# Two feed-forward down projections on one core: Strassen's seven half-block products in place of the plain product, with GpSimd adding the blocks

## What is computed

```python
def conv_ffn(h, w_up, conv_w, conv_b, w_down):
    S = h.shape[1]
    u = h @ w_up                                   # 1024 -> 2 * 2816
    up = jnp.pad(u, ((0, 0), (CONV_W - 1, 0), (0, 0)))
    u = conv_b + sum(conv_w[j] * up[:, j:j + S] for j in range(CONV_W))
    gate, val = jnp.split(u, 2, axis=-1)
    return (jax.nn.silu(gate) * val) @ w_down      # 2816 -> 1024

for layer in range(DEPTH):
    ...
    x = x + m
    x = x + conv_ffn(rms_norm(x, norm_ffn[layer]), f_w_up[layer], ...)
```

## Time and profile before

| | |
|---|---|
| median of 3 runs | 1197.97 us (1197.91 to 1198.34) |
| span of the profiled execution | 1195.8 us; the median of the runs is 2.2 us longer, which lies around the span |
| TensorE busy | 1189.6 us, 99% of the span |
| VectorE, ScalarE, GpSimd busy | 756.1, 561.5 and 202.0 us |
| granted TensorE clock | 1.00 throughout |
| HBM traffic | 96 GB/s over the span |

### The profile page before, as it was taken

How to read it: one execution, slowest core, us unless ns; L and a number is a source line. 1 busy time by engine, 2 the same in 40 slices (tenths; PEclk the granted TensorE clock), 3 DMA queues, 4 the chain that set the end, 5 groups by cost and what they waited for, 6 DMA issues and landing times.

```text
span 1195.8 us, 17325 instructions
## 1 busy us (share of the span) xinstructions
PE 1189.6 (99%) x6082; PEld 974.4 (81%) x6082; DVE 756.1 (63%) x1331; ACT 561.5 (47%) x936; POOL 202.0 (17%) x297
## 2 busy tenths in 40 slices
PE   9999999999999999999999999999999999999998
PEld 7768886778888888888888987988888888888887
DVE  6588967945766566563335998845766566563334
ACT  6554337845433333342225789945443333342321
POOL 0533546820000000000000467720000000000000
PEclk9999999999999999999999999999999999999999
DMA  7522231213332232213232210023332222213232
GB/s 270 185 89 90 71 107 53 73 53 106 110 127 79 105 105 73 102 54 105 90 103 93 88 37 2 2 71 106 107 122 87 105 105 70 105 53 106 88 105 105
DMA packets 26673, 110.84 MB, mean 93 GB/s; under 512 B 2896, under 2 KB 3280, under 8 KB 19456
## 3 DMA queue, kind: packets, MB, share of 16 engines
q1 hardware_dynamic: 26624, 110.21, 27.0%
HBM read 108.06 MB, written 6.33 MB: 96 GB/s over the span
## 4 chain that ended last, share of the span: by engine, by line
PE 97%; ACT 1%; DVE 1%; issue 0%; POOL 0%; DVEq 0%; ACTq 0%; POOLq 0%
PE ps L2164 29%; PE ps L2166 28%; PE ps L2165 28%; PE ps L1931 3%; PE ps L1915 3%; PE ps L1731 1%; PE ps L2130 1%; PE ps L1772 1%; PE ps L1802 1%; PE ps L1899 1%; ACT probs L837 1%; PE ps L1783 0%; PE ps L1739 0%; DVE probs L1308 0%; PE ps L1711 0%
## 5 line engine op out<-in xcount | busy, mean ns | idle before, releaser
L1188 DVE TENSOR_TENSOR w_lo<-raw,w_hi 128x1024 fp32r<-128x1024 f32 (+2 forms) x108 | 179.9, 1665 | 263.0 <-ACT w_hi L747 263.0
L747 ACT ACTIVATE w_hi<-raw 128x1024 fp32r<-128x1024 f32 (+2 forms) x118 | 170.9, 1448 | 222.1 <-PE ps L2166 221.8
L2164 PE MATMUL ps<-h_hi,w_hi 128*128 128x512 f32 x704 | 274.6, 390 | 0.0
L2166 PE MATMUL ps<-h_hi,w_lo 128*128 128x512 f32 x704 | 274.1, 389 | 0.0
L2165 PE MATMUL ps<-h_lo,w_hi 128*128 128x512 f32 x704 | 274.1, 389 | 0.0
L2164 PE MATMUL ps<-a_hi,w_hi 128*128 128x512 f32 x480 | 187.6, 391 | 0.0
L2166 PE MATMUL ps<-a_hi,w_lo 128*128 128x512 f32 x480 | 187.0, 390 | 0.0
L2165 PE MATMUL ps<-a_lo,w_hi 128*128 128x512 f32 x480 | 187.0, 390 | 0.0
L1011 ACT ACTIVATE cv<-u_in,vec 128x512 f32<-128x512 f32 x88 | 71.2, 816 | 182.7 <-DVE u_in L1501 180.6
L2164 PEld LDWEIGHTS ps<-h_hi,w_hi 128*128 128x128 f32 x704 | 132.2, 188 | 28.0 <-issue 0.7
L2165 PEld LDWEIGHTS ps<-h_lo,w_hi 128*128 128x128 f32 x704 | 132.2, 188 | 27.2
(11 more groups left out here) (234 smaller groups left out, 1618.6 us busy)
## 6 DMA issues: line engine op xcount, KB each, us to landing
raw<-in_f_up SPq DMA_DIRECT2D x44, 1024.0 KB, 4.8
raw<-in_f_w_down SPq DMA_DIRECT2D x44, 512.0 KB, 3.3
raw<-in_a_in_wide SPq DMA_DIRECT2D x12, 1024.0 KB, 4.9
bias_tiles<-bias_rows SPq DMA_DIRECT2D x1, 4096.0 KB, 20.3
raw<-in_a_w_out SPq DMA_DIRECT2D x8, 512.0 KB, 3.3
raw<-in_b_w_out SPq DMA_DIRECT2D x7, 512.0 KB, 3.3
xT<-in_xt SPq DMA_DIRECT2D x8, 256.0 KB, 7.0
raw<-in_a_in_wide SPq DMA_DIRECT2D x8, 256.0 KB, 7.1
```

What stands on the lines that cost most here:

```text
L747: sc.activation(w_hi[:, s, 0:n], raw[:, s, 0:n], ACT.Copy).then_inc(w_hi_done, 1)
L1188: dve.tensor_tensor(w_lo[:, s, 0:n], raw[:, s, 0:n], w_hi[:, s, 0:n].bitcast(F32), ALU.subtract)\
L2164: pe.matmul(dst, s_hi, m_hi, start=start, stop=False)
L2166: return pe.matmul(dst, s_lo, m_hi, start=False, stop=stop)
```

## The change

The down projection is computed as a product of 2 x 2 blocks by Strassen's scheme. For each pair of row tiles (even and odd, `G_PAIRS` = 11), the weight has four blocks of 128 rows by 512 output columns and the activation four blocks of 128 rows by 256 tokens. Seven products of sums and differences of blocks (`SEVEN`: column block of the weight, block of the activation, first PSUM bank) take the place of eight plain ones. Each has four matmul triples of 256 columns per pair and gathers in two PSUM banks over the 11 pairs. As seven need 14 banks, there are two phases: units 0 to 10 make M1, M3, M6 and M2, units 11 to 21 load the weights again and make M4, M5 and M7. The last two units run product by product. VectorE adds each finished product onto one or two quarters of the residual, M3 and M2 after ScalarE has copied them to `cv`.

GpSimd makes the sums of the weight blocks in place in the raw slots (three additions of 512 columns in the first phase, two in the second) and sums of the activation blocks (three of 256 per pair), VectorE the other activation sums (two of 256 per pair, in units listed in `SUMMED_IN`). A third raw slot, `raw2`, lies where `h_hi` and `h_lo` lie, so its first load waits until the up projection is done. The first stage of layer 1 takes its weights in eight pieces in a new order and waits for the banks by `g_out`. The semaphores of the feed-forward are shared between the layers.

```diff
+SEVEN = {"M1": (0, 0, 2), "M3": (1, 1, 0), "M6": (2, 3, 4), "M2": (3, 2, 6),
+         "M4": (2, 2, 2), "M5": (0, 1, 0), "M7": (1, 0, 4)}
+G_PAIRS = FT // 2
+G_UNITS = 2 * G_PAIRS
+G_PARTS = ((("M1", "M3"), ("M6", "M2")), (("M4",), ("M5", "M7")))
+SUMMED_IN = {**{i + 2: (i,) for i in range(G_PAIRS - 2)}, 4: (2, 9), 7: (5, 10)}
...
+            raw2 = sb("raw2", [P, SLOT], F32, scope)
...
-                with sp.Fori(0, FT // 2) as i:
-                    for s in range(2):
-                        load(U_DOWN[l] + 2 * i + s, down_v[l][2 * i + s], raw[:, s, 0:D], s)
+                for u in range(G_UNITS):
+                    r, k = u % 3, 2 * pair_of(u)
+                    if u == 2:
+                        sp.wait_ge(f_done, 2 * FT * l + 4 * UP_STEPS)
+                    else:
+                        sp.wait_ge(w_lo_done, U_DOWN[l] + u - (1 if u < 2 else 2))
...
+            def gate_sums(l, i):
...
+                pool.wait_ge(f_act, FT * l + 2 * i + 2)
+                pool.tensor_tensor(g_pair[i][:, 0:HS], even[:, 0:HS], odd[:, HS:S], ALU.add)
+                chain.then_wait(pool.tensor_tensor(g_pair[i][:, HS:S], even[:, HS:S], odd[:, HS:S], ALU.subtract))
+                pool.tensor_tensor(even[:, HS:S], even[:, 0:HS], even[:, HS:S], ALU.add).then_inc(g_pre, 1)
...
+            def weight_sums(l, u):
...
+                pool.wait_ge(g_raw[r], g_landed(l, u))
+                if first_of_two(u):
+                    chain.then_wait(pool.tensor_tensor(s0, s1, s3, ALU.add))
+                    chain.then_wait(pool.tensor_tensor(s3, s2, s3, ALU.add))
+                    pool.tensor_tensor(s2, s2, s1, ALU.subtract).then_inc(g_sum, 1)
+                else:
+                    chain.then_wait(pool.tensor_tensor(s0, s0, s1, ALU.add))
+                    pool.tensor_tensor(s1, s1, s2, ALU.subtract).then_inc(g_sum, 1)
...
+            def sums_of_layer(l):
+
+                for i in range(G_PAIRS - 1):
+                    gate_sums(l, i)
+                for u in range(4):
+                    weight_sums(l, u)
+                gate_sums(l, G_PAIRS - 1)
+                for u in range(4, G_UNITS):
+                    weight_sums(l, u)
...
+            def seven_hi(l, u, p):
...
+                sc.wait_ge(g_sum, G_UNITS * l + u + 1)
+                if u >= 2:
+                    last = 1 if u in (G_PAIRS, G_PAIRS + 1) else p
+                    sc.wait_ge(r_used[1], G_USED * l + 2 * (u - 2) + last + 1)
...
+            def seven_lo(l, u, p):
...
+                dve.tensor_tensor(w_lo[:, s, at], raws[u % 3][:, at], w_hi[:, s, at].bitcast(F32), ALU.subtract)\
+                    .then_inc(w_lo_done if p else g_lo_first, 1)
...
+                dve.tensor_tensor(g_lo[s][:, at], g_source(u, p), g_hi[s][:, at].bitcast(F32), ALU.subtract)\
+                    .then_inc(r_lo[1], 1)
...
+            def gate_differences(l, i):
...
+                chain.then_wait(dve.tensor_tensor(g_diff[:, (i + 8) % G_PAIRS], odd[:, 0:HS], even[:, 0:HS],
+                                                  ALU.subtract))
+                dve.tensor_tensor(odd[:, 0:HS], odd[:, 0:HS], odd[:, HS:S], ALU.add).then_inc(g_diffed, 1)
...
+            def onto(l, count, c, t, source, op):
+
+                x = x_quarter(c, t)
+                dve.wait_ge(g_out, 10 * l + count - 1)
+                dve.tensor_tensor(x, x, source, op).then_inc(g_out, 1)
...
                     elif last:
-                        lo(U_DOWN[l])
-                        act_lo(n, 0, 0)
-                        act_lo(n, 1, 1)
+                        seven_lo(l, 0, 0)
+                        seven_lo(l, 0, 1)
...
-            onto_residual(1, U_DOWN[0], FT)
+            seven_products(0)
...
+                for u in range(G_UNITS - 2):
+                    for p, names in enumerate(G_PARTS[0 if first_of_two(u) else 1]):
+                        wanted(u, p)
...
+                            for d in range(4):
+                                ins = one(name, u, d)
...
+                for name in ("M4", "M5", "M7"):
+                    for u in (G_UNITS - 2, G_UNITS - 1):
```

More of the change, by code:

```diff
@@ L545, in _ @@
             load_ffn(1)
-            for k in range(KD):
-                sp.wait_ge(x_new[4], k + 1)
+            for k in range(4, KD):
+                sp.wait_ge(x_new[4], k // 2 - 1)
                 sp.dma_start(out[:, k, :], xT[:, k, :]).then_inc(out_sem, 16)
-            sp.wait_ge(out_sem, 16 * KD)
+            sp.wait_ge(g_out, 20)
+            for k in range(4):
+                sp.dma_start(out[:, k, HS:S], xT[:, k, HS:S]).then_inc(out_sem, 16)
+            for k in range(4):
+                sp.wait_ge(x_new[4], 3 + k // 2)
+                sp.dma_start(out[:, k, 0:HS], xT[:, k, 0:HS]).then_inc(out_sem, 16)
+            sp.wait_ge(out_sem, 16 * 12)
         @block.gpsimd
@@ L977, in onto_residual @@
                     for b in range(2):
-                        hi(u0 + 2 * i + b + 2, (r_used[n], 2 * i + b + 1), D, b)
+                        hi(u0 + 2 * i + b + 2, (r_used[n], 2 * i + b + 1), D, b, n // 2)
                         act_hi(n, 2 * i + b + 2, b, False)
[L980 to L1000, removed]
@@ new lines, in onto_residual @@
+                half = unit_words(nxt) // 2
+                sc.wait_ge(w_raw[0], 8 * nxt - 16 - (NO_RAW if n else 0))
+                sc.activation(w_hi[:, 0, D:D + half], raw[:, 0, D:D + half], ACT.Copy).then_inc(w_hi_upper, 1)
+                order = ORDER[n_next]
+                for j, k in enumerate(order):
+                    features_hi(n_next, k, gain_at)
+                    if j >= 2:
+                        square_of(n_next, order[j - 2])
+                    if j == KD - 2:
+                        hi(nxt, (r_done[n], KD), half)
@@ L1476, in onto_residual @@
                     dve.tensor_tensor(xT[:, k, :], xT[:, k, :], ps[:, k, :], ALU.add).then_inc(x_new[n_next], 1)
[L1477 removed]
+                    if 0 < j < KD - 1:
                         prepare_lo(n_next, order[j - 1], gain_at)
[L1479 to L1487 removed]
+                lo(nxt, half)
@@ new lines, in into_second_layer @@
+            def into_second_layer():
+                gain_at = G_MIX + KD
+                down_piece_lo(0)
+                down_piece_lo(1)
+                m4_onto_upper(0)
+                onto(0, 8, 0, 0, bank_tiles("M4", 0, 4), ALU.add)
+                prepare_lo(2, 4, gain_at)
+                down_piece_lo(2)
+                dve.wait_ge(g_done, 4)
+                onto(0, 9, 0, 0, bank_tiles("M5", 0, 4), ALU.subtract)
+                onto(0, 10, 0, 1, bank_tiles("M5", 0, 4), ALU.add)
+                prepare_lo(2, 5, gain_at)
+                down_piece_lo(3)
+                prepare_lo(2, 6, gain_at)
+                prepare_lo(2, 7, gain_at)
+                dve.wait_ge(g_out, 10)
+                seven_last(0, 0, 2)
+                seven_last(0, 2, 4)
+                down_piece_lo(4)
+                prepare_lo(2, 0, gain_at)
+                down_piece_lo(5)
+                prepare_lo(2, 1, gain_at)
+                down_piece_lo(6)
+                prepare_lo(2, 2, gain_at)
+                down_piece_lo(7)
+                prepare_lo(2, 3, gain_at)
+                total_squares(2)
@@ L1490, in feed_forward, with into_output @@
+            def into_output():
+                m4_onto_upper(1)
+                onto(1, 8, 0, 0, bank_tiles("M4", 0, 4), ALU.add)
+                dve.wait_ge(g_done, 12)
+                onto(1, 9, 0, 0, bank_tiles("M5", 0, 4), ALU.subtract)
+                onto(1, 10, 0, 1, bank_tiles("M5", 0, 4), ALU.add)
+                seven_last(1, 0, 2)
+                seven_last(1, 2, 4)
             def feed_forward(l):
```

375 lines of the change are left out of this document (296 added, 79 removed).

## The result

The changed kernel takes 1262.14 us (median; 1260.22 to 1263.73) against 1197.97: the ratio is 1.0534, 95% interval 1.0519 to 1.0549. It is slower by 64 us; the forecast was 1245, slower by 47, with a range that reaches to 1275. Direction and place are right, the size is 17 us short.

A forecast was written before the change was run, and what follows sets the result against it. VectorE and GpSimd, excluding each other, bound the down stages: 17 + 63.9 + 56.5 + 4.3 = 141.7 us against 119.7; 2 x 22 + 2.5 = 46.5 on the median 1197.97 gives 1244.5, say 1245; range 1220 to 1275.

The forecast's parts named there:

- TensorE's part: Down projection, per layer: 924 matmuls of 256 columns at 0.12 us, 110.9 us, 8.8 less than before.
- No meeting: Rival, chance 0.10: VectorE's remainders slip into GpSimd's gaps, TensorE bounds the down stages, about 1185 us.
- A meeting: VectorE's two-SBUF-input operation against GpSimd's SBUF-reading one: costs the sum of both steps less 0.35, 1.02 us to VectorE.
- Step 1, the lead: Start of each down stage: VectorE turns to unit 2 about 17 us after the last up matmul.
- Step 2, units 2 to 10: First phase of each down stage: VectorE and GpSimd queues at 7.64 us a unit, 63.9 us after corrections.
- Step 3, units 11 to 21: Second phase of each down stage: 4.72 us a unit plus residual additions, less 3.4 for PSUM reads, 56.5 us.
- starved chain: Rival, chance 0.06: VectorE also waits for loads or ScalarE, one microsecond on each of 20 units, 1285 us.
- Clock: Forecast 1.00 in the down stages; rival, chance 0.03: pauses drop TensorE to 1.2 GHz, steps 0.24 us, about 1400 us.
- Step 4: End of each down stage: TensorE's 36 matmuls after the last remainder, 4.3 us.
- The ends: After the down stages: about 1.5 us of waiting into layer 1 and 1 us more at the output, 2.5 together.
- The gate sums: GpSimd's activation sums of the first ten pairs, during the up steps: 3 x 0.74 us a step, costed at nothing.
- What would show it: Signs: TensorE busy near 94%, idle some 60 us; down windows about 142 us; 1024-column remainders near 2 us; clock 1.00.

The follow-up runs named there:

- fill_sums: Changed kernel with GpSimd filling 1440 columns with a constant for each weight sum, as long at work but reading nothing from SBUF: 1186.11 us.
- extra_sum: Changed kernel with the first weight sum of every first-phase unit made twice, 22 more GpSimd additions of 512 columns: 1282.96 us.
- beside_two_inputs: Kernel before the change, plus two GpSimd 512-column subtractions (both inputs SBUF, spare buffer) per weight tile from the third on in down projections: 1199.62 us.

## Why the prediction was right in direction and short in size

**The mechanism** is as forecast: the two engines take turns. VectorE's and GpSimd's timelines in the changed kernel, at 540:

```profile
540.79 2.28 DVE L1689 TENSOR_TENSOR w_lo<-raw,w_hi 128x1024 fp32r<-128x1024 f32 x1
542.99 1.75 DVE L1693 TENSOR_TENSOR g_lo<-v,g_hi 128x512 fp32r<-128x512 f32 x1
```
```profile
540.40 1.59 POOL L760 TENSOR_TENSOR raw<-raw 128x512 f32<-128x512 f32 x1
542.07 2.12 POOL L761 TENSOR_TENSOR raw<-raw 128x512 f32<-128x512 f32 x1
```

The remainder starts at 540.79 and works only when the addition of 540.40 is through: it ends at 543.07, 1.08 after it. The subtraction of 542.07 waits for the remainder, the next remainder for the subtraction.

**TensorE's part**: 110.9 us forecast, 111.1 busy in fill_sums. Right, with the pace inside a unit of the changed kernel as in the earlier trace rows:

```profile
596.00 0.28 PE L2533 MATMUL ps<-g_hi,w_hi 128*128 128x256 f32 x1
596.12 0.28 PE L2534 MATMUL ps<-g_lo,w_hi 128*128 128x256 f32 x1
```

*No meeting* was priced at "about 1185", and fill_sums, which is that case, gives 1186.1.

**A meeting**: 1.02 us forecast; 0.95 by the tally of the stage and 0.95 by extra_sum. If anything too high, so it is not what was missing. Its premise, that both engines have a backlog as in the earlier trace rows, does not hold: GpSimd works for 91 of 151 us and waits for loads for 46.5 of the rest. The price per sum held all the same, as extra_sum shows.

**Step 1, the lead**: VectorE turns to unit 2 at 550.88, T0 + 17.0, and in layer 1 at 1125.31, T0 + 17.2. Forecast T0 + 17.

**Step 2, units 2 to 10**: 63.9 forecast; the last remainder of unit 10 ends at 618.65, 67.8 us on. **Step 3, units 11 to 21**: 56.5 forecast, 60.5 measured (to 679.19). Together 128.3 for 120.4 in layer 0, and 124.3 in layer 1 (1125.31 to 1249.57). These terms were mis-sized. The step that failed is the sum of both queues as if one of them always had work: VectorE itself stood 6.5 us in the layer 0 stage and 3.2 in layer 1, the rival *starved chain* in small. That is most of the 7.9 and 3.9 us; the other 1.4 and 0.7 are a longer queue of VectorE. The 3.4 us that step 3 gives back for additions that read PSUM were not met in layer 0, where GpSimd was idle beside these additions. The two longest of VectorE's waits stand here, GpSimd, ScalarE, VectorE and TensorE of the changed kernel in turn:

```profile
647.66 5.64 POOL L763 TENSOR_TENSOR raw<-raw 128x512 f32<-128x512 f32 x1 [5.96 <-DMA raw<-in_f_w_down]
```
```profile
654.70 0.63 ACT L1138 ACTIVATE w_hi<-raw 128x512 fp32r<-128x512 f32 x1 [6.38 <-POOL raw L764]
...
667.47 1.06 ACT L1138 ACTIVATE w_hi<-raw 128x1024 fp32r<-128x1024 f32 x1 [5.28 <-PE ps L2535]
```
```profile
650.93 1.22 DVE L1709 TENSOR_TENSOR xT<-xT,cv 128x1024 f32<-128x1024 f32 x1
655.37 1.09 DVE L1689 TENSOR_TENSOR w_lo<-raw,w_hi 128x512 fp32r<-128x512 f32 x1 [3.22 <-ACT w_hi L1138]
...
668.56 1.23 DVE L1689 TENSOR_TENSOR w_lo<-raw,w_hi 128x1024 fp32r<-128x1024 f32 x1 [2.10 <-ACT w_hi L1138]
```
```profile
658.01 0.55 PE L2533 MATMUL ps<-g_hi,w_hi 128*128 128x256 f32 x1 [2.73 <-DVE g_lo L1693]
...
662.69 0.41 PE L2533 MATMUL ps<-g_hi,w_hi 128*128 128x256 f32 x1
...
663.33 0.41 PE L2533 MATMUL ps<-g_hi,w_hi 128*128 128x256 f32 x1
```

At 647.66 a GpSimd sum arrives while VectorE works without a gap until 652.15. The sum, 1.29 us of work, ends at 653.30, 1.15 after that: it was not served in turn, it was shut out. ScalarE needs this unit's sums before its high part (654.70), VectorE needs ScalarE (655.37), and so VectorE, the bound, stands for 3.2 us because of a queue that it had blocked itself. I had put the alternation of the earlier trace rows on every pair; here five VectorE operations in a row (starts at 648.26, 648.86, 649.20, 650.33 and 650.93) passed a waiting sum. What decides between the two orders the runs do not show.

**Clock**: forecast 1.00, measured 0.91 and 0.94 in the stages. From 645 to 655 TensorE works without a gap at a granted clock of 1.00. Then it pauses for 2.73 us, until 658.01; after that it goes at the lower of its two levels, 1.2 GHz:

```profile
658.00:666.00 8.00, 6.98 (x31) 6.73 (x32) 8.00 (x8) 2.96 (x6) 4.80 (x3) 0.50 0.45 141
```

Three matmuls take 0.64 us there (662.69 to 663.33) where they took 0.36 at 596. In the window of 560 to 570 the granted clock is 0.66, while VectorE works for 9.96 of its 10 us. TensorE is busy for 124.7 us in the stage instead of the 111.1 of fill_sums, 13.6 us more. By its place, part of it only fills time in which TensorE would have waited. Part returns through ScalarE, as at 667.47: it waited 5.3 us for TensorE to free a slot, and VectorE then 2.1 us for it. The rival *clock* was right that pauses lower the clock and wrong that it would stay low; its step of 0.24 us is 0.213.

**Step 4**, after the last remainder: 5.4 us for 4.3. **The ends**: 4.6 us into layer 1 and 1.9 at the output for 1.5 and 1. Of these 2.9 and 1.9 are there in fill_sums too, without meetings of the weight sums, so I had taken them too low. In both kernels 2.3 us of the first is one wait of TensorE in layer 1's first stage (before 701.12 here); the profile names no releaser for it, and its cause is not shown. **The gate sums** of the up steps were forecast at nothing, and cost nothing: from layer 1's first up matmul to its first down matmul it is 240.96 us (867.18 to 1108.14) and was 240.94 (831.83 to 1072.77).

**The rest of "What would show it"**: TensorE 95% busy and idle for 61.9 us (forecast 94%, some 60), nearly all in the two stages behind VectorE's remainders; these at 1.65 us (forecast near 2), GpSimd's 512-column additions at 1.6 to 2.1. The 1024-column figure was too high: a remainder that starts first pays nothing (beside_two_inputs), and the 512-column remainders bear more than their part (1.41 for 0.68).

**Slots**: "slots do not bind" holds as far as tried: with three, VectorE waits 6.5 us, and with two another 8.8 us a layer are lost (17.7 in all).

The sum of the misses: in layer 0 7.9 us in steps 2 and 3 and 1.1 in step 4; in layer 1 0.2 in the lead, 3.9 in steps 2 and 3 and 1.2 in step 4; 3.1 and 0.9 at the ends. Together 18.3, and the span grew by 64.8 where 46.5 were forecast. How much of the 7.9 and 3.9 is the shutting out and how much the low clock stays open: no kernel here has the meetings at the full clock. A longer lead of loads or a fourth slot was not tried.

## What to carry to other kernels

When GpSimd reads SBUF beside a VectorE that has two SBUF inputs, add their queues instead of taking the longer; here a 512-column GpSimd sum cost VectorE 0.95 us, and VectorE makes it itself in 0.60. In these runs GpSimd's work cost little or nothing only where VectorE had time to spare (1.9 us in beside_two_inputs), where VectorE read PSUM, or where the GpSimd operation read no SBUF. Before a scheme that trades matmuls for additions is built, run it with the additions taken out: that kernel tells at once the most that the scheme can win, here 7.5 us with the sums cut to 8 columns and 11.4 with fills in their place.

## What the runs showed of the hardware that was not expected

- The operation that starts first is not held up, and the two need not be served in turn; a VectorE without gaps kept GpSimd out for long: 5.64 us for a 1.29 us addition, 7.94 us for a 0.74 us one.
- One SBUF input on GpSimd suffices to hold a VectorE operation up (0.68 to 1.10), though for less than GpSimd's own operation lasts; a fill costs nothing (0.69 in the middle of one, in fill_sums).
- A 256 KB load that adds to SBUF takes 5.9 us to landing beside 3.9 for a plain one in the same kernel, and 58 of them with the plain ones bring the DMA engines to a share of 0.87 at 217 GB/s.
- A pause of 2.7 us in TensorE's work was followed by matmuls at the lower clock (0.50 granted), 0.213 us apart instead of 0.12.
